# Forgetting attention of a streaming encoder: score biases loaded as broadcast tiles and added by VectorE, key transposes in halves, the fold moved

## The reference

```python
def fox_attend(q, k, v, cq, ck, qpos, kpos):
    s = jnp.einsum('bqhd,bkhd->bhqk', q, k).astype(jnp.float32) * (FOX_HEAD_DIM ** -0.5)
    s = s + jnp.swapaxes(cq, 1, 2)[:, :, :, None] - jnp.swapaxes(ck, 1, 2)[:, :, None, :]
    s = jnp.where(kpos[None, :] <= qpos[:, None], s, -jnp.inf)
    p = jax.nn.softmax(s, axis=-1).astype(v.dtype)
    return jnp.einsum('bhqk,bkhd->bqhd', p, v)
```

## Time and profile before

| | |
|---|---|
| runs | 1883.71, 1886.15, 1886.22 us; median 1886.15 |
| profiled execution, span from first to last instruction | 1885.1 us |
| TensorE matmul busy | 1849.9 us, 98% |
| VectorE busy | 983.0 us, 52% |
| ScalarE busy | 722.0 us, 38% |
| GpSimd busy | 225.9 us, 12% |
| attention loops | about 127 to 203 us and 1487 to 1563 us |
| granted TensorE clock | 0.997 of full speed on average |
| DMA | 259 MB, 138 GB/s on average |

### The profile page before, as it was taken

How to read it: one execution, slowest core, us unless ns; L and a number is a source line. 1 busy time by engine, 2 the same in 40 slices (tenths; PEclk the granted TensorE clock), 3 DMA queues, 4 the chain that set the end, 5 groups by cost and what they waited for, 6 DMA issues and landing times.

```text
span 1885.1 us, 29064 instructions
## 1 busy us (share of the span) xinstructions
PE 1849.9 (98%) x12004; PEld 1642.4 (87%) x12004; DVE 983.0 (52%) x1569; ACT 722.0 (38%) x1144; POOL 225.9 (12%) x357
## 2 busy tenths in 40 slices
PE   8999999999999999999999999999999999999998
PEld 8777799998888887799998899998897777999986
DVE  4557653443567778743443664443465576543434
ACT  4246443333255454333332343333242463433321
POOL 3114070000011222230000100000031230000000
PEclk9999999999999999999999999999999999999999
DMA  7357254433353433444433434433364562444332
GB/s 246 128 203 229 81 160 123 129 129 123 117 164 105 125 116 104 118 139 125 124 134 123 146 101 125 132 124 125 110 206 150 200 221 90 137 132 124 128 129 79
DMA packets 179171, 259.38 MB, mean 138 GB/s; under 512 B 14717, under 2 KB 122349, under 8 KB 179040
## 3 DMA queue, kind: packets, MB, share of 16 engines
q1 hardware_dynamic: 161184, 197.18, 32.3%
q0 software_dynamic: 17856, 60.35, 9.9%
HBM read 243.19 MB, written 13.19 MB: 136 GB/s over the span
## 4 chain that ended last, share of the span: by engine, by line
PE 90%; DVE 4%; ACT 3%; issue 1%; DMA 1%; SPq 0%; DVEq 0%; ACTq 0%
PE ps L1605 14%; PE ps L1607 14%; PE ps L1606 14%; PE ps L1617 11%; PE ps L1615 11%; PE ps L1616 11%; PE ps L1833 1%; PE ps L1951 1%; PE ps L1938 1%; PE ps L1638 1%; PE ps L1888 1%; PE ps L1671 1%; DVE w_lo L785 1%; PE ps L1908 1%; PE ps L1673 1%
## 5 line engine op out<-in xcount | busy, mean ns | idle before, releaser
L785 DVE TENSOR_TENSOR w_lo<-w_raw,w_hi 128x1024 fp32r<-128x1024 f32 x370 | 452.1, 1228 | 709.1 <-ACT w_hi L439 707.9
L439 ACT ACTIVATE w_hi<-w_raw 128x1024 fp32r<-128x1024 f32 x370 | 389.3, 1059 | 803.5 <-DMA w_raw<-in_w_ffn_in_dram 363.1
L1605 PE MATMUL ps<-xT_hi,w_hi 128*128 128x384 f32 x1568 | 528.4, 337 | 2.5 <-issue 1.4
L1607 PE MATMUL ps<-xT_hi,w_lo 128*128 128x384 f32 x1568 | 527.0, 336 | 0.0
L1606 PE MATMUL ps<-xT_lo,w_hi 128*128 128x384 f32 x1568 | 526.9, 336 | 0.0
L1605 PEld LDWEIGHTS ps<-xT_hi,w_hi 128*128 128x128 f32 x1568 | 294.8, 188 | 5.2 <-issue 5.1
L1606 PEld LDWEIGHTS ps<-xT_lo,w_hi 128*128 128x128 f32 x1568 | 294.8, 188 | 0.1
L1607 PEld LDWEIGHTS ps<-xT_hi,w_lo 128*128 128x128 f32 x1568 | 294.8, 188 | 0.0
L1617 PE MATMUL ps<-w_hi,hT_lo 128*128 128x512 f32 x528 | 210.6, 399 | 0.0
L1616 PE MATMUL ps<-w_lo,hT_hi 128*128 128x512 f32 x528 | 208.1, 394 | 0.0
L1615 PE MATMUL ps<-w_hi,hT_hi 128*128 128x512 f32 x528 | 207.4, 393 | 0.0
(11 more groups left out here) (329 smaller groups left out, 2021.8 us busy)
## 6 DMA issues: line engine op xcount, KB each, us to landing
w_raw<-in_w_ffn_in_dram SPq DMA_DIRECT2D x352, 256.0 KB, 3.2
w_raw<-in_w_ffn_out_dram SPq DMA_DIRECT2D x176, 256.0 KB, 2.9
w_raw<-in_w_fox_in_dram SPq DMA_DIRECT2D x96, 256.0 KB, 2.9
k_c<-in_cache_fox_k_dram POOLq DMA_DIRECT2D x32, 512.0 KB, 5.3
v_c<-in_cache_fox_v_dram POOLq DMA_DIRECT2D x32, 512.0 KB, 4.0
w_raw<-in_w_hgrn_in_dram SPq DMA_DIRECT2D x64, 256.0 KB, 2.9
w_raw<-in_w_fox_out_dram SPq DMA_DIRECT2D x32, 256.0 KB, 2.9
out_dram<-kv_tok POOLq DMA_DIRECT2D x4, 1024.0 KB, 5.0
```

Source lines behind the costliest of these rows:

```text
L439: nc.scalar.activation(w_hi[:, slot, :], w_raw[:, slot, :], ACT.Copy).then_inc(hi_ready, 1)
L785: V.tensor_tensor(w_lo[:, slot, :], w_raw[:, slot, :], w_hi[:, slot, :].bitcast(F32), ALU.subtract).then_inc(lo_ready, 1)
L1605: mm(out, w_hi[:, slot, cols], x_hi[:, k, :], start=k == 0, stop=False, skip_group_check=True)
L1607: last = mm(out, w_lo[:, slot, cols], x_hi[:, k, :], start=False, stop=k == KD - 1, skip_group_check=True)
```

## The change

- TensorE's bias and mask products are gone, and with them `c_p`, `c_s`, the selectors, the mask rows and VectorE's split at units 17 and 18. The sums keep their sign, the queries are scaled by -SCALE instead, so all scores are negated.
- After the scans SyncE stores `cp` and `craw` to DRAM scratch (four stores), waits for their landing, and loads them back broadcast over the partitions: `bias_p` (two prompt heads, 128 x 2 x 384, two buffers) and `bias_s` (one stream, each row over the 16 queries of its head, 128 x 2 x 272, two buffers). The first two of each are loaded ahead of the first output-projection weights, the other 12 during the loop, each after the one before has landed and VectorE is done with its buffer.
- GpSimd subtracts the mask from every loaded bias: the first four ahead of the loop, the others in `next_mask`, at the end of its turn n of the K and V loop (m = n - 3 from 2 to 13): an even m masks the prompt biases m // 2 + 1, an odd m the sample biases (m + 1) // 2.
- VectorE adds bias and scores and takes the minimum in one instruction (`tensor_tensor_reduce`), into `p_s` and `p_p` in SBUF; ScalarE's exponentials read these. The next scores wait for this instruction and no longer for the exponential.
- In `s_keys` half of the key transposes stand ahead of `s_turn`, the other half behind it. `s_fold` moves from the head of the step into the middle of `p_scores` or `p_out`.
- VectorE scales the prompt weights ahead of the low part of the folded output; ScalarE's sample exponential goes ahead of the high part.

The diff, cut to its core:

```diff
@@ SyncE
+            def first_biases(i, j):
+                f = FOX[i]
+                sync.wait_ge(*at(f["c"], 1 + DB))
+                sync.dma_start(sums_p[j, :, 0:P], cp[:, 0:P]).then_inc(f["bias_in"][0], 16)
+                sync.dma_start(sums_p[j, :, P:T], cp[:, :]).then_inc(f["bias_in"][0], 16)
+                for hf in range(2):
+                    sync.dma_start(sums_s[j, :, :, hf, :], craw[8 * hf:8 * hf + 8, :, :]).then_inc(f["bias_in"][0], 16)
+                sync.wait_ge(*at(f["bias_in"], LOADED))
+                for k in range(2):
+                    prompt_bias_in(i, j, k)
+                for b in range(2):
+                    sample_bias_in(i, j, b)
+            def prompt_bias_in(i, j, k):
+                sync.dma_start(bias_p[:, k % 2, :, :], sums_p[j, 2 * k:2 * k + 2, :].partition_broadcast(P)).then_inc(
+                    FOX[i]["bias_in"][0], 16)
+            def sample_bias_in(i, j, b):
+                sync.dma_start(bias_s[:, b % 2, :, :],
+                               sums_s[j, :, b, :, :].rearrange("h f k -> h (f k)").unsqueeze(1).broadcast_to(
+                                   [HEADS // 2, DT, 2 * (PAST + DT)])).then_inc(FOX[i]["bias_in"][0], 16)
+            def next_bias(i, j, t):
+                f = FOX[i]
+                sync.wait_ge(*at(f["bias_in"], LOADED + 16 * (3 + t)))
+                if t % 2:
+                    sync.wait_ge(*at(f["nmax"], t + 1))
+                    prompt_bias_in(i, j, t // 2 + 2)
+                else:
+                    sync.wait_ge(*at(f["s_nmax"], t))
+                    sample_bias_in(i, j, t // 2 + 1)
...
-                    chunks(w_fox_out[j], s["out"], 2)
+                    first_biases(i, j)
+                    chunks(w_fox_out[j], s["out"], 2, 0, RING)
+                    for t in range(1, 2 * DB - 3):
+                        next_bias(i, j, t)
+                    chunks(w_fox_out[j], s["out"], 2, RING)
@@ ScalarE
                 for n in range(HEADS + 3):
+                    if 1 <= n <= HEADS:
+                        act.wait_ge(*at(f["s_nmax"], n))
+                        nc.scalar.activation(p_s[:, (n - 1) % 2, :], p_s[:, (n - 1) % 2, :], ACT.Exp,
+                                             bias=nmx[:, (n - 1) % 2, 2:3], scale=-1.0, accum_out=rs[:, (n - 1) % 2, 2:3]).then_inc(f["s_exp"][0], 1)
@@ VectorE
                         dve.wait_ge(*at(f["s_scores"], n))
-                        V.tensor_reduce(nmx[:, (n - 1) % 2, 2:3], ps[:, SS_BANK, 0:PAST + DT], AX_X, ALU.max,
-                                        negate=True).then_inc(f["s_nmax"][0], 1)
+                        if n % 2:
+                            dve.wait_ge(*at(f["bias"], sample_bias(n // 2)))
+                        V.tensor_tensor_reduce(out=p_s[:, (n - 1) % 2, :], in0=ps[:, SS_BANK, 0:PAST + DT],
+                                               in1=bias_s[:, (n - 1) // 2 % 2, (n - 1) % 2, :], scale=1.0, scalar=LARGEST, op0=ALU.add,
+                                               op1=ALU.min, accum_out=nmx[:, (n - 1) % 2, 2:3]).then_inc(f["s_nmax"][0], 1)
...
-                        V.tensor_reduce(nmx[:, n % 2, 0:1], ps[:, bank, 0:P], AX_X, ALU.max, negate=True)
-                        V.tensor_reduce(nmx[:, n % 2, 1:2], ps[:, bank, P:T], AX_X, ALU.max,
-                                        negate=True).then_inc(f["nmax"][0], 1)
+                        if n % 2 == 0:
+                            dve.wait_ge(*at(f["bias"], prompt_bias(n // 2)))
+                        for q, lo, hi in ((0, 0, P), (1, P, T)):
+                            ins = V.tensor_tensor_reduce(out=p_p[:, n % 2, lo:hi], in0=ps[:, bank, lo:hi],
+                                                         in1=bias_p[:, n // 2 % 2, n % 2, lo:hi], scale=1.0, scalar=LARGEST, op0=ALU.add,
+                                                         op1=ALU.min, accum_out=nmx[:, n % 2, q:q + 1])
+                        ins.then_inc(f["nmax"][0], 1)
@@ GpSimd
+                def next_mask(m):
+
+                    pool.wait_ge(*at(f["bias_in"], LOADED + 16 * (3 + m)))
+                    if m % 2:
+                        mask_sample_bias((m + 1) // 2)
+                    else:
+                        mask_prompt_bias(m // 2 + 1)
+
                 pool.wait_ge(*at(f["kT_a"], KD))
+                pool.wait_ge(*at(f["bias_in"], LOADED + 16 * 4))
+                for k in range(2):
+                    mask_prompt_bias(k)
+                for b in range(2):
+                    mask_sample_bias(b)
...
                     if n - KV + 2 < 2 * DB:
                         load_new(n - KV + 2)
+                    if 2 <= n - KV < 2 * DB - 2:
+                        next_mask(n - KV)
@@ TensorE
                 def p_scores(k):
-                    for e in range(2):
-                        h = 2 * k + e
-                        if k:
-                            pe.wait_ge(*at(f["exp"], h - 1))
-                        out = ps[:, S_BANK[e], 0:T]
-                        mm(out, sel_p[:, h:h + 1].broadcast_to([CROWS, P]), c_p[:, :], start=True, stop=False, skip_group_check=True)
-                        mm(out.rearrange("p (t c) -> p t c", t=NTOK)[:, 0:NTOK:2, :], ident_r[:, :],
-                           causal_r[:, :].rearrange("p (t c) -> p t c", t=NTOK)[:, 0:NTOK:2, :], start=False, stop=False,
-                           skip_group_check=True)
+                    if k:
+                        pe.wait_ge(*at(f["nmax"], 2 * k))
                     for lo, hi, n in ((0, P, P), (P, T, SEQ)):
+                        if lo and k:
+                            s_fold(2 * k - 2)
...
-                    mm(ps[:, SS_BANK, 0:PAST + DT], sel_s[:, n % 2, :], c_s[:, n // 2, :], start=False, stop=True,
-                       skip_group_check=True).then_inc(f["s_scores"][0], 1)
...
                 for n in range(HEADS + 1):
-                    if n >= 2:
-                        s_fold(n - 2)
...
-                    if n == 1:
-                        s_keys(n, KT_BANKS)
+                    if 1 <= n < HEADS:
+                        s_keys(n, KT_BANKS, range(2))
...
-                    if 2 <= n < HEADS:
-                        s_keys(n, KT_BANKS)
                     if 1 <= n < HEADS:
+                        s_keys(n, KT_BANKS, range(2, 4))
                         p_turn(n - 1)
```

151 lines of the change are left out of this document (72 added, 79 removed).

## The result

The changed kernel takes 1920.4 us (median of four runs, 1918.9 to 1921.8); the kernel before, beside it on the same chip, 1885.05. The ratio is 1.0188, its 95% interval 1.0175 to 1.0201: 35 us slower, where 1880.5 was forecast and 1892 was the upper end. In the profiled executions the spans are 1918.6 and 1885.1 us, 33.5 apart. Further down, three single executions (2045 us in e13, 5333 in e15, 5556 in e16) ran far longer than all others; the ratios leave them out, the medians of the table count them.

What follows compares the result with a forecast made beforehand. TensorE's order of work was taken as the loop's bound. Shorter pairs, less a late first K load and mask waits, gave 2.8 us a layer, 5.6 in two: 1880.5 us median, own range 1877 to 1884, full range 1869 to 1892.

Steps and rivals of the forecast that it cites:

- SyncE's other new waits: Ahead of the loop, four stores and their landing before the first output-projection weights: cost nothing, at worst 1 to 2 us.
- the clock is no term: Granted clock 1.00 in all attention stretches read of the kernel before, so no cost was counted for it.
- the 9.2 of the forecast: In the loop, a pair of steps with masks takes 9.2 us, against 9.55 before; six such pairs, the last 8.5.
- Rival (d): Broadcast bias transfers move at half the rate of others: 11.2 us a pair, 1905 us in all; chance 0.05.
- 4.0 us a step: TensorE's work left in either loop step once products and waits go: 8.0 us a pair against 9.55.
- The forecast's reason for the halves: In the odd step, without key transposes in halves and the moved fold, TensorE's 0.17 us wait would be 0.3 to 0.4.
- The sample mask: GpSimd's late mask delays VectorE on the even head's sample scores: the odd step takes 5.2 us instead of 4.0.
- Rival (b): GpSimd's prompt mask blocks VectorE's scaling in the even step: TensorE waits 0.4 us, 1885 us in all; chance 0.12.
- Transfers of 9.0 to 9.2 a pair: In the loop, 2.83 MB a pair takes 9.0 to 9.2 us, as long as the pair, holding nothing mid-loop.
- The start of the loop: Late K load puts step 3's sample scores at 142.35 us, 142.13 before: the first pair's gain is gone.
- The vector operation: VectorE's fused add and minimum on sample scores: about 0.43 us for 272 columns, plus an accumulator read of 0.05 to 0.1.
- rival (c): Fused vector op takes half as long again as a plain one: 9.85 us a pair, 1888 us; twice, 1897; chance 0.18.

Runs made afterwards that it cites:

- e13: e9 with two thirds of each prompt bias load, and GpSimd's prompt mask waiting until VectorE has scaled that step's prompt weights; 1883.8 us, ratio 0.9991.
- e15: e14 with the fold back at the start of the step, key transposes still in halves; 1875.5 us, ratio 0.9948.
- e16: e15 with key transposes in one piece, so TensorE's order is that of the kernel before; 1873.0 us, ratio 0.9930.
- e1: Changed kernel with the first two loads of out-projection weights between the four stores and the wait for their landing; 1904.5 us, ratio 1.0113.
- e8: e5 without any of GpSimd's masks in the loop, VectorE waiting for each bias landing instead; 1888.5 us, ratio 1.0018.
- e14: e1 with the first four bias tiles used for all heads, no bias loaded or masked in the loop; 1877.4 us, ratio 0.9965.
- e12: Kernel before with only the change's order: key transposes in halves, fold between halves of prompt products, ScalarE and VectorE to match; 1894.1 us, ratio 1.0036.
- e7: e5 without GpSimd's masks on the prompt biases loaded in the loop; 1891.7 us, ratio 1.0040.
- e5: e1 plus a semaphore of its own for each bias buffer, so issues no longer wait for the landing before; 1900.1 us, ratio 1.0077.
- e18: e13 with the fold at the start of the step and key transposes in one piece, TensorE's old order; 1882.1 us, ratio 0.9986.
- e9: e5 with GpSimd's masks ahead of its other waits and loads, and step 3's K load ahead of the V stores; 1894.5 us, ratio 1.0047.

## Why the prediction was wrong

**Failed first: "SyncE's other new waits ... Cost nothing, at worst 1 to 2 us".** They cost 7.8 and 9.6 us, by the marks (in layer 3 about 2 of that may be scatter), and e1 takes 16 us off the median. I named the stores and their landing, and left out the four bias loads of 1.3 MB that stand in the same queue ahead of the weights, in issue time and on the DMA engines. I also took ScalarE's in-order wait to have "some units" of slack; of the 9.97 us that ScalarE waited, only 4.4 were slack. The drop of the clock behind the stall, about 1.6 and 2.4 us, was in no term ("the clock is no term"): the forecast read it in a kernel without stalls.

**Failed second: the price of next_bias.** The forecast summed bytes and treated each landing as hidden, though the diff lets each issue wait for the landing before it. Ten landings in series at 5.7 us are 57 us, and the first two, at 8.5 and 7.5, make it 73. A near price was at hand: the K loads of half a MB landed in 5.3 us as a median in the kernel before, and the late one in 8.1. Two landings of 5.3 are longer than the 9.2 of the forecast. Rival (d) had the size (11.2 a pair) with the wrong cause: broadcast loads are not at half rate, e8 moves 301 GB/s with them.

**Failed third: 4.0 us a step.** Measured 4.41 and 4.31 (e14). The products taken away were priced rightly (1.23), and so were the halves. The new order was costed at a gain, from rows of another order: the fold at 0.14 although has 0.26 for it in the odd step, and nothing for the products that it now cuts in two. By e14's rows the missing 0.72 a pair are the fold (0.36 in both steps, + 0.44) and the cut products (1.06 for 0.86 and 0.95 for 0.88, + 0.27). The same order in the kernel before measures + 0.42 a pair (e12). The forecast's reason for the halves, that without them the wait of 0.17 would grow to 0.3 to 0.4, is refuted by the 0.03 of e16.

**Right, but hidden.** The sample mask: "the odd step takes 5.2 instead of 4.0"; e7, with it as the only wait, has 5.25 against 4.31. Rival (b), the prompt mask against VectorE's scaling, said + 0.4 a pair; e5 against e7 gives 10.1 against 9.7. In my forecast I gave it 0.12, yet in e5 six of the six masked pairs in layer 0 show it (scalings of 2.1 us); its chance should have been higher, since GpSimd's order puts the two at the same moment in every even step. Transfers of 9.0 to 9.2 a pair: 9.15 and 9.43 in e8, behind the first pair. The start of the loop: sample scores of step 3 were forecast 9.8 us behind step 1 and came 9.6 behind it (150.04), with the K load as the wait; as this step 1 was 7.8 us late, the nearness is in part luck (e1, e5 and e8, with step 1 in time, have 10.8 to 13.2). The vector operation was 442 ns for 0.43, the read 83 ns for 0.05 to 0.1: rival (c) is refuted. By the Trainium skill ("VectorE: DVE Perf Modes", section "Two Vector instructions with no wait between them") such an operation is two instructions, and the rows of L1049 show the two.

With terms one and two put away (e5: 1900.1) the time is still 20 us above the forecast: 12 are pairs of 10.1 against 9.2 and a last one of 9.6 against 8.5 (the third term and rival (b) together), 4 the first pairs (13.2 and 10.8 us against 9.8), and the rest lies outside the loops.

**Left open.** The fold's new place costs 0.68 us a pair in the kernel before and only 0.17 with the new arithmetic (e14 against e15). The rows show where: at the start of the step it takes 0.14 and 0.26 in the first case, and twice 0.36 with a wait of 0.09 in the second. Why the same two products take 0.14 in one place and 0.36 in another they do not show. What holds VectorE's scaling before the mask's row begins is open too. That masks done by another engine, or bias loads spread over fewer bytes, would beat e18 was not tried.

## What to carry to other kernels

When a change puts transfers in a queue, write down for each of them what it waits for, what is queued behind it, and who waits for that in order; a wait for "the one before has landed" makes a chain whose price is landings, not bytes. Price moved work by a row from its new neighbourhood, or as unknown: a matmul group that is cut or put between others can cost two or three times its old rows. Where several costs lie beside each other, the longest hides all the rest, so removing one shows the next: here serial landings at about 11, then masks at 10.1, then transfers near 9.4, then TensorE at 8.7. And where single executions scatter by several us outside the stage that a change touches, read its effect from that stage's own marks, with the granted clock beside them.

## What the runs showed of the hardware

- In a stall of TensorE of 5.6 us its granted clock fell, and stayed at 0.50 (1.2 GHz) for some 3 us of renewed work (some 5 behind 5.2 us in layer 3). Inside the loop it was 0.87 over a pair with waits of 2.8 us (e5), and 0.73 over the pair behind a wait of 2.6 us (e9).
- With the DMA engines at 0.93 over the loop and 0.99 in its fullest stretch (301 GB/s, e8), half-MB K loads landed in 8.9 us as a median instead of 5.3. A quarter of these bytes are broadcast loads; without them the fullest stretch of the kernel before moved 314 GB/s.
- A 128x256 scaling, SBUF to SBUF, beside GpSimd's 128x512 operation took up to 2.4 us instead of 0.35, and was held although that operation's row began 1 us later; a semaphore that let GpSimd start only after it took the hold away and shortened the two loops by 3.6 us, without moving the recorded starts.
- Fold products of 128x64 took 0.14, 0.26 or 0.37 us by what stood around them.
